# Feed-forward loop with all four groups of k tiles by seven block products, one weight sum per group made by an accumulating DMA

## The reference, cut to what matters

```python
def swiglu(x, w_gate, w_up, w_down):
    return (jax.nn.silu(x @ w_gate) * (x @ w_up)) @ w_down

x = x + 0.5 * swiglu(rmsnorm(x, ffn1_norm[l]), ffn1_w_gate[l], ffn1_w_up[l], ffn1_w_down[l])
...
x = x + 0.5 * swiglu(rmsnorm(x, ffn2_norm[l]), ffn2_w_gate[l], ffn2_w_up[l], ffn2_w_down[l])
```

## Time and profile before

| | before |
|---|---|
| time, median of 3 runs | 2042.21 us (2042.13 to 2042.24) |
| span of the profiled execution | 2040.2 us |
| PE busy | 2027.8 us, 99% of the span |
| DVE busy | 1858.9 us, 91% |
| ACT busy | 1267.5 us, 62% |
| POOL busy | 87.6 us, 4% |

### The profile page before, as it was taken

The page is one execution under the profiler, slowest core; times in us unless marked ns, Lnnn a source line. Parts: engine busy times, 40 slices in busy tenths (PEclk is TensorE's granted clock), DMA queues, the critical chain, the costliest instruction groups (busy, mean ns, idle before and its releaser), DMA issues.

```text
span 2040.2 us, 26364 instructions
## 1 busy us (share of the span) xinstructions
PE 2027.8 (99%) x9204; PEld 1678.7 (82%) x9204; DVE 1858.9 (91%) x1897; ACT 1267.5 (62%) x1474; POOL 87.6 (4%) x80
## 2 busy tenths in 40 slices
PE   9999999999999999999999999999999999999998
PEld 7888888888888888888888888888888888888886
DVE  7999999999999798887689999799999999999997
ACT  7666666666666556666556556466666666666664
POOL 0000000000000000000000000000000000000000
PEclk9999999999999999999999999999999999999999
DMA  8578777787877455554536575655878777877773
GB/s 301 206 211 259 230 236 246 227 236 227 246 247 235 157 186 183 198 177 157 183 134 227 189 243 182 211 186 192 242 223 250 244 232 211 260 225 240 247 231 127
DMA packets 222143, 441.03 MB, mean 216 GB/s; under 512 B 7648, under 2 KB 7824, under 8 KB 221936
## 3 DMA queue, kind: packets, MB, share of 16 engines
q1 hardware_dynamic: 202112, 401.64, 56.1%
q0 software_dynamic: 19744, 38.28, 11.3%
q10 hardware_dynamic: 208, 0.08, 0.0%
HBM read 400.13 MB, written 2.10 MB: 197 GB/s over the span
## 4 chain that ended last, share of the span: by engine, by line
PE 98%; DVE 1%; ACT 0%; DMA 0%; issue 0%; SPq 0%; ACTq 0%; DVEq 0%
PE ps L765 16%; PE ps L767 16%; PE ps L766 16%; PE ps L778 12%; PE ps L780 12%; PE ps L779 12%; PE ps L1002 2%; PE ps L1003 2%; PE ps L1001 2%; PE ps L1050 2%; PE ps L1052 2%; PE ps L1051 2%; PE ps L856 1%; PE ps L834 0%; DMA xres<-in_x 0%; PE ps L1169 0%
## 5 line engine op out<-in xcount | busy, mean ns | idle before, releaser
L1788 DVE TENSOR_TENSOR w_lo<-raw,w_hi 128x1024 fp32r<-128x1024 f32 x280 | 337.9, 1219 | 7.2 <-ACT w_hi L1356 4.9
L1356 ACT ACTIVATE w_hi<-raw 128x1024 fp32r<-128x1024 f32 x280 | 290.8, 1053 | 72.6 <-PE ps L767 54.0
L1356 ACT ACTIVATE w_hi<-sums 128x1024 fp32r<-128x1024 f32 x160 | 169.8, 1063 | 204.8 <-PE ps L767 71.4
L1788 DVE TENSOR_TENSOR w_lo<-sums,w_hi 128x1024 fp32r<-128x1024 f32 x160 | 195.3, 1222 | 33.8 <-ACT w_hi L1356 31.1
L765 PE MATMUL ps<-w_hi,hT_hi 128*128 128x512 f32 x536 | 208.8, 390 | 0.0
L767 PE MATMUL ps<-w_hi,hT_lo 128*128 128x512 f32 x536 | 208.5, 389 | 0.0
L766 PE MATMUL ps<-w_lo,hT_hi 128*128 128x512 f32 x536 | 208.5, 389 | 0.0
L1788 DVE TENSOR_TENSOR more_lo<-raw,more_hi 128x1024 fp32r<-128x1024 f32 x140 | 169.2, 1219 | 6.6 <-ACT more_hi L1356 5.6
L765 PE MATMUL ps<-w_hi,xT_hi 128*128 128x512 f32 x424 | 170.1, 401 | 0.0
L1356 ACT ACTIVATE more_hi<-raw 128x1024 fp32r<-128x1024 f32 x140 | 146.4, 1054 | 32.6 <-PE ps L767 23.8
L767 PE MATMUL ps<-w_hi,xT_lo 128*128 128x512 f32 x424 | 165.7, 391 | 0.0
(11 more groups left out here) (366 smaller groups left out, 5007.4 us busy)
## 6 DMA issues: line engine op xcount, KB each, us to landing
raw<-in_ffn_w_up SPq DMA_DIRECT2D x88, 1024.0 KB, 5.5
raw<-in_ffn_w_down SPq DMA_DIRECT2D x88, 1024.0 KB, 5.3
raw<-in_ffn_w_gate SPq DMA_DIRECT2D x87, 1024.0 KB, 5.4
raw<-in_w_in SPq DMA_DIRECT2D x80, 1024.0 KB, 5.0
xres<-gate_buf POOLq DMA_DIRECT2D x72, 512.0 KB, 5.5
raw<-in_w_out SPq DMA_DIRECT2D x16, 1024.0 KB, 5.1
raw<-in_w_proj_dil SPq DMA_DIRECT2D x8, 1024.0 KB, 5.5
raw<-in_w_proj_fox SPq DMA_DIRECT2D x8, 1024.0 KB, 5.2
```

The source lines that it names most:

```text
L1356: nc.scalar.activation(slot_hi(place, offset), src, ACT.Copy).then_inc(hi_ready, 1)
L1788: nc.vector.tensor_tensor(slot_lo(place, offset), step_source(r)[0], slot_hi(place, offset).bitcast(F32), ALU.subtract).then_inc(lo_ready, 1)
```

## The change

- The fourth group also goes by seven products, so a step has four pairs (at 0, 7, 14 and 21) and then the down slabs (28 to 35): 36 slabs. `direct_up` and the direct slabs are gone.
- Signs of the scheme are turned, so that all weight sums are additions (the tokens' sums and a factor -1 in `rstd_q` take them up).
- The order within a pair is now T3, gate 0, T2, up 1, T1, T4, gate 1. The sum T1 is no longer made by DVE: POOL issues a DMA that adds the gate rows onto the up rows in `raw` (`add_t1`). It waits for T3 (which reads the same up rows) and for the load of the gate block. ACT waits for its landing (`t1_added`) before it rounds slab 4 of the pair.
- DVE makes T3 of the next pair ahead of the split of slab 4, T2 ahead of the split of slab 2 and T4 ahead of the split of slab 3.
- Once per feed-forward block, DVE and ACT prepare the token sums of the fourth group.

```diff
-FIRST, STEP = 2 * WIDE, 33
+FIRST, STEP = 2 * WIDE, 36
...
-PAIR_AT, PAIR_GROUPS, PAIR_SLABS = (0, 7, 18), (1, 2, 3), 7
-PAIRS = len(PAIR_AT)
-DIRECT_AT, DIRECT_GROUP = 14, 0
+PAIR_AT, PAIR_GROUPS, PAIR_SLABS = (0, 7, 14, 21), (1, 2, 3, 0), 7
+PAIRS, PAIR_FOURTH = len(PAIR_AT), 3
...
+FFN_PRODUCTS = (("sum", T3), ("gate", 0), ("sum", T2), ("up", 1), ("sum", T1), ("sum", T4), ("gate", 1))
+FFN_SUMS = (T3, T2, T4)
...
+            def add_t1(f, q, pair):
+
+                up_l, gate_l = PAIR_LOADS[pair]
+                place = step_place(f, q)
+                pool.wait_ge(summed, f * SUMS + q * SUMS_STEP + len(FFN_SUMS) * pair + 1)
+                pool.wait_ge(raw_landed[gate_l % LOADS], place.landed(gate_l))
+                pool.dma_start(raw[:, up_l % LOADS, 0::2, :], raw[:, gate_l % LOADS, 0::2, :],
+                               accum_op=ALU.add).then_inc(t1_added[pair], 16)
...
+            for f in range(2):
+                add_t1(f, 0, 0)
+                add_t1(f, 0, 1)
+                for q in range(STEPS):
+                    add_t1(f, q, 2)
+                    add_t1(f, q, 3)
+                    if q < STEPS - 1:
+                        add_t1(f, q + 1, 0)
+                        for n in range(3):
+                            add_down(f, q, n)
+                        add_t1(f, q + 1, 1)
+                        add_down(f, q, 3)
...
-                if kind == "paired" and o in (1, 2, 4):
-                    weight_sum(place, q, pair, {1: T1, 2: T2, 4: T4}[o], count)
-                if r + 1 in PAIR_AT:
-                    weight_sum(place, q, PAIR_AT.index(r + 1), T3, count)
-                if r == STEP - 1 and not final:
+                if kind == "paired" and o == 2:
+                    weight_sum(place, q, pair, T2, count)
+                if kind == "paired" and o == 3:
+                    weight_sum(place, q, pair, T4, count)
+                if kind == "paired" and o == 4 and pair + 1 < PAIRS:
+                    weight_sum(place, q, pair + 1, T3, count)
+                if r == STEP - 2 and not final:
                     weight_sum(place, q + 1, 0, T3, count)
                 dve.wait_ge(hi_ready, place.slab(offset + 1))
                 nc.vector.tensor_tensor(slot_lo(place, offset), step_source(r)[0],
...
-                        if o == 22:
+                        if o == 24:
                             dve.wait_ge(combined, merged + 1)
-                            nc.vector.tensor_tensor(u3, ps[:, M7], u2, ALU.add).then_inc(combined, 1)
-                        if o == 23:
+                            nc.vector.tensor_tensor(u3, ps[:, F_M7], u2, ALU.add).then_inc(combined, 1)
+                        if o == 25:
+                            dve.wait_ge(slab_done, place.slab(25))
                             dve.wait_ge(combined, merged + 2)
+                            nc.vector.tensor_tensor(u2, ps[:, F_UP0], u2, ALU.add).then_inc(combined, 1)
```

More of the change, by code:

```diff
@@ L399, in step_source @@
         if kind == "paired":
-            what, which = PRODUCTS[o]
+            what, which = FFN_PRODUCTS[o]
+            up_l, gate_l = PAIR_LOADS[pair]
+            if what == "sum" and which == T1:
+                return raw[:, up_l % LOADS, 0::2, :], None
             if what == "sum":
-                return sums[:, SUM_PLACE[which]], None
-            l = PAIR_LOADS[pair][what == "gate"]
+                return sums[:, FFN_PLACE[which]], None
+            l = gate_l if what == "gate" else up_l
             return raw[:, l % LOADS, which::2, :], l
-        l = DIRECT_LOADS[o // 2] if kind == "direct" else DOWN_LOADS + o // 2
+        l = DOWN_LOADS + o // 2
         return raw[:, l % LOADS, o % 2 * 2:o % 2 * 2 + 2, :], l
@@ L476, in build @@
     summed = sem("summed")
+    t1_added = [sem(f"t1_added{n}") for n in range(PAIRS)]
+    fourth_x_ready = sem("fourth_x_ready")
     s_ready = sem("s_ready")
@@ L646, in load_group @@
                         load_step(place, l, w[f][:, CT * g:CT * (g + 1), cols])
[L648 removed]
+                    for pair in range(PAIRS):
                         load_group(PAIR_LOADS[pair][0], PAIR_GROUPS[pair], up_w)
                         load_group(PAIR_LOADS[pair][1], PAIR_GROUPS[pair], gate_w)
[L651 to L654, removed]
                     for n in range(NN):
@@ L947, in step @@
                     pe.wait_ge(ht_lo, hid + 1)
[L948 to L954, removed]
+                    transpose_tokens(hid, 1, F_TURN)
                     for o in paired(place, 2):
                         pass
+                    pe.wait_ge(s_lo, (f + 1) * PAIRS)
+                    for o in paired(place, PAIR_FOURTH):
+                        pass
+                    pe.wait_ge(ht_lo, hid + TT)
                     for n in range(NN):
-                        pe.wait_ge(combined, merged + (1, 3, 4, 5)[n])
+                        pe.wait_ge(combined, merged + (1, 2, 4, 5)[n])
                         if last and n == NN - 1:
@@ L989, in ffn @@
                     end_down(last_place(f), HID[f] + STEPS * TT, ADDED[f] + NN)
[L991 to L1004, removed]
             def transpose_dil(n):
@@ L1464, in step @@
                     for o in range(STEP):
-                        if last and o == 26:
+                        if last and o == 29:
                             act.wait_ge(combined, merged + 5)
@@ L1938, in step @@
                     for o in range(STEP):
-                        if o == 22:
-                            dve.wait_ge(slab_done, place.slab(22))
-                            dve.wait_ge(m1_copied, i + (f * STEPS + 1))
-                            nc.vector.tensor_tensor(u2, ps[:, M6], partial[:, PART_M1],
-                                                    ALU.add).then_inc(combined, 1)
-                        if last and o == 25:
+                        if last and o == 28:
                             gate_sum(place)
-                        if last and o == 26:
+                        if last and o == 29:
                             dve.wait_ge(combined, merged + 4)
-                            multiply_up([up_sums[:, 1 - t] for t in range(TT)], i * TT + (silu + TT))
+                            multiply_up([up_sums[:, 1 - t] for t in range(TT)], i * TT + (silu + TT), rstd_q)
                         if not last or o + FFN_RING < STEP:
@@ L1965, in step @@
                               .then_inc(combined, 1)
-                        if o == 24:
-                            dve.wait_ge(slab_done, place.slab(23))
-                            dve.wait_ge(combined, merged + 3)
-                            nc.vector.tensor_tensor(up_sums[:, :, :], ps[:, UP1:UP1 + TT],
-                                                    up_sums[:, :, :], ALU.add).then_inc(combined, 1)
-                        if not last and o == 26:
+                        if not last and o == 28:
@@ L1972, in step @@
                             gate_sum(place)
-                        if not last and o == 28:
+                        if not last and o == 31:
                             dve.wait_ge(combined, merged + 4)
-                            multiply_up([up_sums[:, 1 - t] for t in range(TT)], i * TT + (silu + TT))
+                            multiply_up([up_sums[:, 1 - t] for t in range(TT)], i * TT + (silu + TT), rstd_q)
                         if last and o == DOWN_AT + 3:
-                            split_hidden(hid + TT, last_lo, last_hi, GATE)
+                            split_hidden(hid + TT, last_lo, last_hi, F_GATE)
```

169 lines of the change are left out of this document (99 added, 70 removed).

## The result

The changed kernel takes **2203.6 us** (median of 4 runs, 2197.7 to 2205.4) against 2042.2 us before: ratio 1.0785, interval 1.077 to 1.080. It is 161 us slower. I had forecast 2147 us, with 2180 as the upper end of the range: the sign is right, the size is not, and the measured time lies outside.

A forecast was written before the change was run, and what follows sets the result against it. DVE replaces PE as the bound: 61.1 plain work + 5.2 T2 waits + 1.0 ring = 67.3 us a step against 62.17, +103 us over 20 steps; with 2 once per block and 2.0 to the median, 2147 us, range 2130 to 2180.

The forecast's parts named there:

- 6 matmuls less a step: On PE, 48 matmuls become 42; worth 1.36 us a step, 27 us in all, only if PE stays the bound.
- DVE's plain work: DVE's splits, weight sums, combinations and gate product in one step, without waits: 61.1 us, against PE's 60.8.
- T2's wait: DVE idles between T2 and its split while ACT rounds: 1.3 us a pair, 5.2 us a step.
- the ring: DVE waits at the end of the six-slab ring while PE works on the down slabs: about 1.0 us a step.
- Once per block: Fourth group's token sums, outside the regular steps: 1 us for each of two blocks, 2 us in all.
- The T1 add "at nothing": T1's sum as an accumulating DMA from POOL: landing by 7.9 us, needed at 12.7, so costed at nothing.
- the 4.8 us of cover: Spare time of each T1 add before ACT must round its slab; each us beyond it at all pairs costs 80 us.
- DMA would be at 90%: Twelve loads and eight adds need 60.4 us of DMA time in a 67.3 us step.
- late transfers: Rival: T1's add or a load comes late; 2171 us at one pair a step, 2243 at all four; 16%.
- the second rival: Prediction's phrase where transfers from all queues share the same 16 DMA engines, so each add also lengthens the loads around it.
- some 86%: Case of the late-transfers rival: DMA share cannot go above this, a step takes 70.2 us, the kernel 2205 us.
- The trap of starved descriptors: GpSimd-issued DMAs starve for descriptors while DVE runs a two-port instruction, making T1 late; the prediction's rows spoke against it.

The follow-up runs named there:

- the kernel with both edits: Changed kernel, with POOL issuing a step's first `xres` add ahead of the next pair 0's T1 add, and T2 made one split earlier: 2127.1 us, ratio 1.040.
- the one without T1 adds: Changed kernel with the first `xres` add issued ahead of the T1 add, T2 one split earlier, and all T1 adds left out: 2092.5 us, ratio 1.025.

## Why the prediction was wrong in size

- **PE.** 6 matmuls less a step is right, and worth nothing, as forecast: PE waits.
- **DVE's plain work, 61.1 us; T2's wait, 1.3 a pair; the ring, 1.0.** Right. The kernel without the T1 adds has 67.29 us a step; T2 to its split is 2.42 us; the longest ring wait in that step is 0.63. The time was 2153, 6 us over my 2147, and that is the next term.
- **Once per block, 2 us.** Too small: 9 us stand outside the steps, 4.5 a block. I had 0 to 4.7 for a block and took 1, since DVE would start the loop with its ring full. The trace has 4.1 us of this work within the first step, with nothing to hide it.
- **The T1 add "at nothing".** This is the step that failed; measured, the adds cost 51 us. I priced an add only by the wait for its own landing, with a landing (5.5 us) taken from a kernel with four adds a step. With eight it is 7.7 (9.8 in the step shown). That alone would have stayed within the 4.8 us of cover at the median, and ACT's direct waits for T1 are only 16.6 us in all. But in the step shown the add also had to wait for its gate block and took 10.6 us to land: from T3's start (325.19) to its landing (340.1) are 15.0 us, where I had 7.9 at the most and 12.7 allowed. And the larger part of the cost falls on the transfers beside it (next point). I had worked out myself that DMA would be at 90% of 67.3 us, and then priced each transfer as if alone.
- **What was left out of the sum.** The `xres` adds were there before and I treated them as unchanged. They went from 5.5 to 10.8 us, and ACT's copy waits for them directly (61.4 us). The gate loads went from 5.4 to 8.1 and the up loads from 5.5 to 6.3, and DVE waits for the up loads (15.5 us). I looked at POOL's queue for what delays T1 and not for what T1 delays.
- **The rival that came in** is the first, late transfers, which I gave 16% with 2171 to 2243 us. Its mechanism was right in kind; I had put most of its weight near 2170, on one pair a step. The measured price is 51 us. (Where the prediction gives the shared DMA engines as the reason for "the second rival", it is this one that is meant.) One of its cases, a DMA share that cannot go over some 86%, gives 2205 us, and 2203.6 was measured; that is luck. No row showed 86%, and the kernel with both edits ran at 0.92.
- **The trap of starved descriptors** does not show: POOL's T1 issues are 1.26 us long on average, `xres` 1.30, for 1.18 before. T1 is late after its issue. DVE's splits and sums are all `TENSOR_TENSOR` here; whether any instruction of the kind that the warning is about ran beside an issue, no row shows.

## What to carry to other kernels

When work moves from a compute engine to DMA, add up the DMA engines' time first, and if their share rises clearly (here from 0.77 to 0.85 in a step), do not price a transfer by its landing in the old trace: look at everything that waits for any transfer in that stretch, the old ones too. The share alone is no price: the kernel with pair 0's T1 on DVE ran at 0.90 over its loops and was 12 us over the one without T1 adds, the changed kernel at 0.88 and 51 over its own. In a queue that works in order, ask what a new entry that must wait holds up behind it, as well as what holds it up. And in a program written in order, a value that another engine must round should have at least one other instruction between its making and its use: here one line moved was worth 55 us in the changed kernel and 60 without the T1 adds.

## What the runs showed of the hardware

- An accumulating DMA is dear for its size: 0.5 MB takes 3.1 us of all 16 engines' time (34.3% of the 72.8 us step for eight), a plain load of 1 MB 3.0 us (50.2% for twelve). In the earlier trace rows it is 3.1 and 2.9. Nor does its price go with its bytes: the adds of 16 columns in 512 have 1/32 of them in as many packets, and still take about 1.2 us each (15.4% of 2152.9 us, less 3.1 for each of the 80 T1 adds, for 72; an estimate).
- Crowded DMA goes with uneven times. Kernels with eight large adds a step spread over 8 to 24 us from run to run; those without T1 adds by DMA, over 1 to 4.
- The GpSimd addition of two SBUF operands held DVE: 3.44 us for an instruction of 1.22.
- A hand-over between engines is short: 0.11 us from DVE's end to ACT's start (T2 ends at 334.72, ACT starts at 334.83), 0.03 from ACT's end to DVE's start (335.89 and 335.92, in the step shown after the result). T2's wait is nearly all ACT's own 1.06 us and DVE's unfinished 0.09.
